# A hybrid attention and delta-rule layer on one Trainium2 core: level zero of the recurrence ahead of the last convolution taps, the last root on VectorE, weight splits in three parts

## The reference, cut to what matters

```python
h = rms_norm(x, norm_g)
proj = h @ w_in                                  # mixers' inputs, and 3 x 1024 merge gates
# A: top-128 keys by an indexer, softmax attention over them
# B: causal conv (4 taps) + silu on q, k, v; gated delta rule in chunks:
a_mat = where(strict, (k_beta @ k.T) * decay, 0)
t_inv = triangular_solve(eye + a_mat, eye)       # inverse of a unit triangular matrix
v_new = t_inv @ (...) ; o = q @ state + attn @ v_new ; state = decay * state + k.T @ v_new
o_b   = rms_norm(o, b_out_norm) * silu(b_z)
# C: compressed + selected + window attention, each gated
merged = g_a * (y_a @ wb_a) + g_b * (y_b @ wb_b) + g_c * (y_c @ wb_c)
out = x + merged @ w_out
```

## Time and profile before

| | us |
|---|---|
| median of 3 runs (lowest, highest) | 652.02 (651.27, 655.02) |
| the profiled execution: its time, its span | 654.71, 652.6 |
| busy: TensorE, VectorE, ScalarE, GpSimd | 589.1 (90%), 394.3 (60%), 333.5 (51%), 222.6 (34%) |
| granted TensorE clock, mean over the span | 0.974 |
| chain that ended last | PE 67%, DVE 14%, ACT 8%, issue 5%, POOL 2%, DMA 2% |

### The profile page before, as it was taken

How to read it: one execution, slowest core, us unless ns; L and a number is a source line. 1 busy time by engine, 2 the same in 40 slices (tenths; PEclk the granted TensorE clock), 3 DMA queues, 4 the chain that set the end, 5 groups by cost and what they waited for, 6 DMA issues and landing times.

```text
span 652.6 us, 10019 instructions
## 1 busy us (share of the span) xinstructions
PE 589.1 (90%) x3763; PEld 368.8 (57%) x3763; DVE 394.3 (60%) x889; ACT 333.5 (51%) x585; POOL 222.6 (34%) x161
## 2 busy tenths in 40 slices
PE   3969988999999996999999999988988799799998
PEld 2424556756548653677677777754554466333443
DVE  6401487451687965786876557447799765577311
ACT  4625654425688768350812525346766677243510
POOL 0133453333044466042531530422221464242520
PEclk9998999989999899799999999979999999999999
DMA  8254764443113232120211110111120211162411
GB/s 321 63 127 111 155 123 130 138 153 113 51 50 113 66 98 65 33 65 2 65 33 32 53 46 1 46 53 51 36 78 34 66 33 43 56 228 74 145 55 48
DMA packets 31168, 53.04 MB, mean 81 GB/s; under 512 B 2743, under 2 KB 13201, under 8 KB 31121
## 3 DMA queue, kind: packets, MB, share of 16 engines
q1 hardware_dynamic: 30961, 52.27, 27.7%
q10 hardware_dynamic: 160, 0.14, 0.1%
HBM read 49.98 MB, written 2.42 MB: 80 GB/s over the span
## 4 chain that ended last, share of the span: by engine, by line
PE 67%; DVE 14%; ACT 8%; issue 5%; POOL 2%; DMA 2%; SPq 2%; DVEq 0%; ACTq 0%; PEldq 0%; POOLq 0%
PE bank L1790 12%; PE bank L1603 10%; PE bank L1605 9%; PE bank L1604 9%; PE bank L1858 5%; PE bank L1860 5%; PE bank L1862 5%; ACT stage L735 3%; PE bank L1639 2%; DMA stage<-in_w_in 2%; PE bank L1682 2%; POOL w_lo L518 1%; PE bank L1988 1%; PE bank L1821 1%; PE bank L1761 1%
## 5 line engine op out<-in xcount | busy, mean ns | idle before, releaser
L518 POOL TENSOR_TENSOR w_lo<-stage,w_hi 128x1024 f16<-128x1024 f32 (+4 forms) x76 | 149.1, 1964 | 250.9 <-ACT w_hi L743 250.9
L1790 PE MATMUL bank<-work 128*128 128x128 f32 x616 | 80.1, 280 | 8.1 <-DVEq L1298 7.8
L1790 PEld LDWEIGHTS bank<-work 128*128 128x128 f32 x616 | 77.7, 195 | 17.1 <-DVEq L1298 9.9
L743 ACT ACTIVATE w_hi<-stage 128x1024 f16<-128x1024 f32 (+4 forms) x76 | 74.5, 981 | 18.8 <-issue 14.4
L735 ACT ACTIVATE stage<-stage,small 128x512 f32<-128x512 f32 (+4 forms) x120 | 73.6, 662 | 8.1 <-DMA stage<-in_w_in 8.0
L1858 PE MATMUL bank<-hT_hi,w_hi 128*128 128x512 f16 x192 | 74.5, 388 | 1.7 <-PE bank L1862 0.9
L1860 PE MATMUL bank<-hT_lo,w_hi 128*128 128x512 f16 x192 | 74.2, 387 | 0.5 <-PE bank L1605 0.2
L1862 PE MATMUL bank<-hT_hi,w_lo 128*128 128x512 f16 x192 | 74.1, 386 | 0.3 <-PE bank L1605 0.2
L1603 PE MATMUL bank<-w_hi,hT_hi 128*128 128x260 f16 (+4 forms) x192 | 62.7, 327 | 9.1 <-POOL w_lo L518 6.4
L1604 PE MATMUL bank<-w_lo,hT_hi 128*128 128x260 f16 (+4 forms) x192 | 62.5, 326 | 0.0
L1605 PE MATMUL bank<-w_hi,hT_lo 128*128 128x260 f16 (+4 forms) x192 | 62.5, 325 | 0.0
(11 more groups left out here) (319 smaller groups left out, 1183.6 us busy)
## 6 DMA issues: line engine op xcount, KB each, us to landing
stage<-in_w_in SPq DMA_DIRECT2D x40, 512.0 KB, 3.5
stage<-in_c_phi_w SPq DMA_DIRECT2D x8, 512.0 KB, 4.0
stage<-in_w_branch SPq DMA_DIRECT2D x8, 512.0 KB, 3.7
stage<-in_w_out SPq DMA_DIRECT2D x8, 512.0 KB, 3.8
stage<-in_w_in SPq DMA_DIRECT2D x8, 260.0 KB, 2.8
strips<-rel_rows SPq DMA_DIRECT2D x8, 256.0 KB, 7.3
late<-in_x SPq DMA_DIRECT2D x1, 2048.0 KB, 10.1
out_x<-late SPq DMA_DIRECT2D x8, 256.0 KB, 2.0
```

Source lines behind the costliest of these rows:

```text
L518: gp.tensor_tensor(piece_view(w_lo[:, k % PAIRS, :], c), piece_view(stage[:, piece_at[c, j] % STAGES, :], c), piece_view(w_hi[:, k % PAIRS ...
L743: nc.scalar.activation(piece_view(w_hi[:, k % PAIRS, :], c), full, ACT.Copy).then_inc(hi_ready, 1)
L1790: ins = mm(ps[:, h * P:(h + 1) * P], lhs(h), rhs(h), start=True, stop=True)
```

## The change

Seven edits.

- **Level zero first.** The four transposes `("n", 0)` move from behind the fill at the head of the recurrence into the last tile of B2, behind its fifth step. On VectorE `decayed_products(0)` and `level_zero(0)` stand before convolutions 9, 10, 11, whose taps become a generator at the head of `topk_last`, taken one at a time in levels 1 to 3; four top-k steps stand before `decayed_products(0)`, eight more before the log decays. On ScalarE the SiLUs of 9 to 11 and the first tap of 11 move behind the three gate SiLUs (L907).
- **token_major(0)** moves from level 3 to level 5.
- **The last root** (`("ob", 3)`) is found on VectorE from a bit pattern and three Newton steps (`bit_root`, 13 small instructions), and the whole last norm moves from ahead of unit 0 into unit 2.
- **Entry of the attention:** the compressed products move into unit 0, and 12 fill steps (`FILL_FIRST`, three times 4) stand among them; block 3 units have 4 fill steps and not 5.
- **Splits in three parts:** ScalarE scales row 0, row 1 and rounds in three different units; GpSimd's part follows the rounding.
- **finish(g)** a unit earlier (`u % 4 == 2`), without the copy L1493.
- **Top-k rounds** of the attention by `ROUNDS_AT`, from unit 3 on, 7 in 8 units.

```diff
-TOPK_0, TOPK_A, TOPK_B = 10, 16, 6
+TOPK_0, TOPK_A, TOPK_B, TOPK_C = 10, 24, 6, 4
-ATTENTION_FILL = (7, 7, 5, 5)
+ATTENTION_FILL = (7, 7, 5, 4)
+FILL_FIRST = 4
+ROUNDS_AT = (1, 1, 0, 1, 2, 1, 0, 1)
...
-        def attention_splits(u):
-            g = 12 + u // 4
-            c = GATE_CHUNKS[g // 4]
-            if g % 4 == 3:
-                return [(after(c), 2 + u % 4 - 1)] if u % 4 in (1, 2) else []
-            return [(after(c), g % 4)] if u % 4 == 3 and g % 4 < 2 else []
+        SPLIT_PARTS = {0: (0, "row0"), 1: (0, "row1"), 2: (0, "hi"), 4: (1, "row0"), 5: (1, "row1"), 6: (1, "hi"),
+                       8: (2, "row0"), 9: (2, "row1"), 10: (3, "row0"), 12: (3, "row1"), 13: (2, "hi"), 14: (3, "hi")}
+        def attention_split(u):
+            j, part = SPLIT_PARTS.get(u % 16, (None, None))
+            return after(GATE_CHUNKS[3 + u // 16]), j, part
...
-                else:
+                elif t < 3:
                     first_tap(8 + t)
-                silus(t, {1: (8,), 2: (9,), 3: (10, 11)})
+                silus(t, {1: (8,)})
...
             ins.then_inc(z_ready, 1)
+            silu_conv(9)
+            first_tap(11)
+            silu_conv(10)
+            silu_conv(11)
...
-            sqrt(("ob", NT - 1), ss_o[:, 4 * NT - 4:4 * NT], 4)
...
+            def bit_root(ss, n):
+                y, w = root[:, 0:n], newton[:, 0:n]
+                bits = y.bitcast(i32)
+                hold(ve.tensor_scalar(bits, ss.bitcast(i32), 1, None, ALU.arith_shift_right))
+                hold(ve.tensor_scalar(bits, bits, -1.0, ROOT_SEED, ALU.mult, ALU.add))
+                for n in range(3):
+                    hold(ve.tensor_tensor(w, y, y, ALU.mult))
+                    hold(ve.tensor_tensor(w, w, ss, ALU.mult))
+                    hold(ve.tensor_scalar(w, w, -0.5, 1.5, ALU.mult, ALU.add))
+                    if n < 2:
+                        hold(ve.tensor_tensor(y, y, w, ALU.mult))
+                return y, w
...
             difference(0)
             conv(8)
-            conv(9)
+            for _ in range(TOPK_C):
+                next(topk_last)
             decayed_products(0)
-            conv(10)
             level_zero(0)
-            conv(11)
+            topk_last = chain(conv_taps(9), conv_taps(10), conv_taps(11), topk_last)
...
-                elif m == "sel":
-                    hold(ve.tensor_copy(oc, o_cg[:, 4 * q:4 * q + 4, :]))
                 if m != "A":
+                    before = o_cg[:, 4 * q:4 * q + 4, :] if m == "sel" else oc
...
-            for _ in output_norm(NT - 1):
-                pass
-            cmp_out()
-            last_rounds = topk(3)
             for u in range(len(units)):
                 if u + 2 < len(units):
                     logits(u + 2)
                 probs_lo(u)
-                next(last_rounds, None)
+                if u == 0:
+                    cmp_out(0)
+                elif u == 1:
+                    cmp_out(1)
+                elif u == 2:
+                    for _ in output_norm(NT - 1):
+                        pass
+                    last_rounds = topk(3)
+                else:
+                    for _ in range(ROUNDS_AT[u % 8]):
+                        next(last_rounds, None)
                 for f in Y_EARLY.get(u, ()):
                     y_lo(f)
-                if u % 4 == 3 and u >= 7:
+                if u % 4 == 2 and u >= 6:
                     finish(u // 4 - 1)
...
+                if (t, k) == (3, 4):
+                    GD.wait(pe, ("nnt", 0))
+                    transposes(("n", 0), [neg_nT[:, h, :] for h in range(4)])
...
             fill(2 * FILL_T)
-            GD.wait(pe, ("nnt", 0))
-            transposes(("n", 0), [neg_nT[:, h, :] for h in range(4)])
...
-                    if l == 3 and c == 0:
+                    if l == 5 and c == 0:
                         pe.wait_ge(conv_done, 12)
                         token_major_inputs(0)
...
             unit_logits(0)
+            fill(FILL_FIRST)
             unit_logits(1)
+            fill(FILL_FIRST)
...
                 if u + 2 < len(units):
                     unit_logits(u + 2)
+                if u == 0:
+                    compressed_out(0)
+                    fill(FILL_FIRST)
+                    compressed_out(1)
```

More of the change, by code:

```diff
@@ L691, in _ @@
             for u in range(len(units)):
-                for c, j in attention_splits(u):
+                c, j, part = attention_split(u)
+                if part == "hi":
                     lo_split(c, j)
@@ L1208, in conv @@
                         hold(ins)
-                ins.then_inc(conv_ready, 1)
+                    else:
+                        ins.then_inc(conv_ready, 1)
+                    yield
+            def conv(m):
+                for _ in conv_taps(m):
+                    pass
             for t in range(4):
@@ L1336, in output_norm @@
                 hold(ve.tensor_reduce(so, o_sq, AX.X, ALU.add))
-                ve.tensor_scalar(so, so, 1.0 / B_HD, EPS, ALU.mult, ALU.add).then_inc(ROOT_IN.sem, 1)
-                yield
-                y, w = newton_root(("ob", c), so, 4)
+                ins = ve.tensor_scalar(so, so, 1.0 / B_HD, EPS, ALU.mult, ALU.add)
+                if c < NT - 1:
+                    ins.then_inc(ROOT_IN.sem, 1)
+                    yield
+                    y, w = newton_root(("ob", c), so, 4)
+                else:
+                    hold(ins)
+                    y, w = bit_root(so, 4)
                 yield
```

51 lines of the change are left out of this document (36 added, 15 removed).

## The result

The changed kernel takes 656.56 us (median of 15 runs, 653.81 to 657.66), the kernel before on the same chip 652.56 (15 runs). The ratio is 1.0046, 95% interval 1.0033 to 1.0060: slower by 3.0 us by the ratio and by 4.0 between the medians, which by the ratio is just within the 0.5% that a measurement can tell from no change; the whole interval lies above 1, so the change does not gain. Forecast were 640.7 us, a gain of 11.3. The profiled execution of the changed kernel took 656.08 (span 654.0).

The account below looks back on a forecast made before the run. TensorE, busy 90% of the span, was taken as the bound, VectorE in units 16 to 31. Gains 6.7 + 2.0 + 2.6 = 11.3 us from the median 652.0 gave 640.7; 631 to 646 held about 0.82.

Parts of the forecast that it names:

- The entry with units 0 and 1: Start of the attention: 4.9 us of waits and slow clock removed, 0.4 added waiting for the first exponential.
- slow units 0 and 1: Attention entry: 6.5 us at mean clock 0.54 hold 3.5 of full clock, so 2.9 us removed.
- Part A: Level zero first, between B2 and the recurrence: gain of 6.7 us (4 to 9).
- the gain of A comes back in B2: Rival: extra top-k delays log decays, TensorE waits in B2: 644 us; 0.22 shared with the clock rival.
- Part C: The attention's units 8 to 47: gain of 2.6 us, summed from −3.4, +0.3, +2.5 and +3.2.
- waits of pieces 2 and 3: Units 13 and 14: TensorE waits 2.3 and 2.5 us for late-rounded pieces, together 4.8 lost.
- The blocked product: Small VectorE product of `finish` beside GpSimd's rest: 0.8 us each in units 6, 18, 22, 34 (bounds 0 and 1.8).
- Units 32 to 47: Last units: some 4.5 us of waits, leaving one blocked `finish` 0.8 and 0.5 at the end: gain 3.2.
- Part B: Entry of the attention and the moved norm: 4.9 − 2.9 = 2.0 us gained, if the clock stays up.
- the clock falls again at the entry: Rival: a slow stretch like the old one at the attention's entry, 2.9 us, 643.6; 0.22 shared with the B2 rival.
- The norm: Unit 2, VectorE, 4.4 us at one go: TensorE waits 2.5 for `probs_lo(3)` in unit 4 (bounds 1 and 3.5).
- Slower than before: Rival: scattered waits keep the clock at 1.2 GHz, deciding above 23 us there; 30 us gives 656; chance 0.03.

Follow-up runs that it names:

- ac_gate: Parts A and C on the kernel before, with ScalarE draining gate tile 0 ahead of the split queued with it: 643.04 us, ratio 0.9849.
- A and C: The changed kernel with Part B undone (norm and root ahead of the units, no FILL_FIRST): 644.84 us, ratio 0.9875.
- no lead: The changed kernel without the 12 FILL_FIRST fill steps, ATTENTION_FILL back to 7, 7, 5, 5: 651.63 us, ratio 0.9983.
- products first: The changed kernel with both groups of narrow compressed products ahead of unit 0, the last FILL_FIRST between them: 652.38 us, ratio 0.9989.
- norm in unit 0: The changed kernel with the last norm in unit 0, not unit 2 (also written norm_u0): 654.18 us, ratio 1.0005.
- table early: The changed kernel with one small exponential on ScalarE behind the last cp drain, to load the table early: 653.67 us, ratio 0.9994.
- pieces early: The changed kernel with the split parts of pieces 2 and 3 of the first block moved to units 8 to 12: 654.47 us, ratio 1.0006.
- late `finish`: finish back at u % 4 == 3: in the changed kernel 651.18 us, ratio 0.9971; added to ac_gate 637.01 us, ratio 0.9739.
- A alone: Only Part A on the kernel before, attention entry and units as before: 647.73 us, ratio 0.9918.
- A and B: The changed kernel with Part C undone (whole splits, copy kept, a top-k round a unit, finish a unit later): 659.38 us, ratio 1.0096.
- ac_lead: ac_gate with late `finish`, 10 fill steps moved to the entry from units 32 to 41, pieces 2 and 3 split early: 635.19 us, ratio 0.9704.

## Why the prediction was wrong

Predicted 640.7, with a range of 631 to 646; measured 656.6, or 652.02 × 1.0046 = 655.0 from the median that the forecast started from, a miss of 14.3 us. "Slower" and "the same" together had a chance of 0.08. Two of the three parts came out near their sums (A 1.4 under, C 0.2 to 0.7 over, C partly by luck); B has the miss of 13 to 14.

**The steps that failed.** Profile against profile, the miss is 12.7 (641.3 forecast for the span of 654.0), and it lies in three places. *The entry with units 0 and 1* was put at 4.9 − 0.4 = 4.5 shorter and is 16.91 − 12.79 = 4.1 longer: the term "slow units 0 and 1" was taken as removed on the condition that the clock stays up, and the clock was 0.70; the table load was in no term. *Units 32 to 46* were put at 3.2 shorter and are 0.6 longer (37.38 for 36.80). *The tail* is 1.6 longer at a low clock that no term had. What is left, among it the 1.6 won ahead of B2's last tile, makes −1.3.

**Part A: 6.7 forecast, 5.3 measured by the ratio (4.9 between the medians), 6.2 by both traces up to the first logits.** Right step by step. The wait in B2, ahead of the `n` transposes at 250.79, was 0.61 (forecast 0.5); VectorE's product ended at 249.95 + 0.69 = 250.64, 1.5 earlier than forecast, and TensorE was there earlier by as much. Level 1 starts at 254.80 and runs at the full clock (its matmuls of 512 columns start 0.215 apart). The bank wait of gate tile 0 was 2.12, forecast 2.1, and its cause, ScalarE's order, is shown by ac_gate. The rival "the gain of A comes back in B2" is out.

**Part C: 2.6 forecast, 2.8 and 3.3 measured, and yet wrong inside.** The forecast had −4.8 for the waits of pieces 2 and 3 in it. They came (2.38 and 2.48, for 2.3 and 2.5), but they belong to B's lead: with A and C alone they are absent. C by itself was thus forecast at 7.4 and gave 2.8; that the sum of 2.6 was met is luck. Two steps failed, and a stretch at the low clock came on top (0.92 over the 20.96 of units 16 to 23 in A and C, some 1.7; with gate tile 0 drained first the same units take 19.39 at 1.00):
- *The blocked product.* It was priced at 0.8 in four places, 3.2. All six candidates were hit, with 10.13 − 6 × 0.166 = 9.1 us more on VectorE (1.74 + 1.33 + 1.72 + 1.66 + 2.07 + 1.61 = 10.13), and removing them is worth 4.9 to 7.2. The mechanism was right; the value was taken in the lower half of its bounds, as if the two might miss each other. They don't: in every kernel with the rounding and `finish` in the same six units (A and C, no lead, products first, norm in unit 0, table early, gate tile first) the six products last 1.3 to 2.1. In the code both hang on the same unit's transposes. It is timing all the same: in "pieces early" piece 3 is rounded in unit 12 and the product of unit 14 takes 0.17, and in unit 10, where piece 2's rounding and `finish` now meet, the product (462.19) starts 0.04 before GpSimd's rest (462.23) and takes 0.17 too. The Trainium skill, page "SBUF — State Buffer", section "Who interferes with whom", has an exclusive lock for the pair; by the page alone each would cost up to the whole 2.13, and the six, 1.33 to 2.07, lie nearer to that than to my 0.8. The trace agrees with the page.
- *Units 32 to 47 at +3.2.* They gave −0.9 in A and C (20.15 to 21.05 in 32 to 39, and 16.65 both times in 40 to 46). The forecast took the waits "behind the finish of the top-k" as gone, and did not ask when the top-k ends: with 7 rounds in 8 units the 32 steps last to unit 36, and from unit 3 on to unit 37; before, they ended in unit 31. That is by the code; in the windows of units 32 to 39 VectorE does one step of the top-k before, five in A and C and seven in the changed kernel, 0.68 each. VectorE's busy time in units 32 to 39 went from 12.79 to 17.10 and to 18.48. The late `finish` brings the stretch to 19.02 and VectorE's busy time to 14.90.

Units 24 to 31 were forecast at +2.5 and gave 3.2, as VectorE's row said.

**Part B: 2.0 forecast, −11.2 to −11.6 measured.** With the waits for the pieces booked here, forecast −2.8. Its terms, from the windows of A and C against those of the changed kernel:
- *The entry, forecast 4.5 shorter.* Against A and C it is 16.91 − 12.66 = 4.25 longer, so the step has a miss of 8.75. An estimate of its terms from the first window: the clock, 16.91 × (1 − 0.70) = 5.1, forecast 0; idle time, 16.91 − 15.46 = 1.45, forecast 0.4; and the 12 fill steps, 12 × 0.214 = 2.6, forecast as covered. The rival "the clock falls again at the entry" was priced at 2.9, as a stretch like the old one; it happened, and was longer than the old one (0.70 over 16.91 against 0.73 over 12.79). The narrow products took 2.98 + 3.67 = 6.65 where 32 in one go took 3.78 in A alone: 2.9. The first exponential stood behind its table load of 1.28, which starts only when its logits are there. Undoing the order alone gave 3.7 by the ratio; its stretch up to unit 2 is 3.2 shorter, as no lead's is 3.2 longer than that of A and C (15.87 and 12.66).
- *The 12 fill steps themselves.* Priced at nothing ("a hole that four fill steps cover", "1.7 of the old 23.9 were fill steps that moved"). The entry is 1.04 shorter without them (no lead), since 1.5 of their 2.6 fill idle time; given back are 0.5 in units 40 to 46 and 0 to 0.65 in 24 to 31. So the price of nothing was right to within half a us. What they cost is the two waits for pieces 2 and 3, which they pull forward; those were forecast, but not as B's.
- *The norm.* A wait of 2.25, forecast 2.5, and right in cause: norm_u0 removes 2.26. What was not seen is that 7.9 us of idle time lay on VectorE in unit 0, ahead of the place where it was put.
- *Units 8 to 15:* 25.67 − 19.10 = 6.57, of it 4.86 the two waits, forecast 4.8; the rest is mostly a stretch at the low clock directly behind them (0.94 over 8 to 15, an estimate of 1.5), which no term had.
- Back comes 2.2 in units 16 to 23, where A and C had its own low stretch (0.92) and a blocked product.

4.25 + 2.26 + 6.57 − 2.22 + 0.04 + 0.22 − 0.54 = 10.6, and 1.0 outside these stretches: 11.6, the difference of the two profiled spans (654.0 − 642.4). The medians stand 11.7 apart.

**The rivals.** "Slower than before" named the clock alone, decided above 23 us at the low level. That count did not come: by the mean clocks of the windows about 13.6 us of the stretch from 419.15 to 494.17 lay at the low level (2 × 0.30 × 16.91, 2 × 0.06 × 25.67, 2 × 0.01 × 18.74), worth 6.8. It was more than half of the way, though, and joined by what had no rival with a chance of its own: an uncovered table load and a top-k that ends late, at nothing in the sum, and `finish` blocked at six places of six, priced low. The range's lower side was filled with waits being absent; but the waits of A, of the pieces and of the norm were all there, at their size to within 0.3 us.

**Open:** why the clock falls where it does in the entry. The same order on TensorE took 15.37 at a mean of 0.78 (norm in unit 0), 16.91 at 0.70 (changed kernel, A and B) and 18.32 at 0.64 (pieces early, late `finish`), one profiled execution each, and the narrow products in them took 1.99 to 3.14 and 2.96 to 3.67. So the slow time at the entry isn't set by the order alone, and how much of B's 11.7 another execution would show is not settled. The executions of norm_u0 and table_early spread over 8.6 and 10 us, those of A and C over 0.7. By the ratios the single repairs of 4.1 (no lead), 3.7 (products first), 2.7 (norm) and 3.4 (table) sum to 13.9, more than B's 11.2; at equal clock they sum to 9.7 to 11.6, and products first and table early remove the same wait. No run separates the bit root from the move of the norm, or in C the parts of the splits from the direct use of `o_cg`.

## What to carry to other kernels

Filler work that is moved has two prices, one at each end: read how much idle time it lands in (here 1.5 of 2.6), and from what stretch it is taken; one whose TensorE row is nearly full gave back 1.26 of 1.7 (ac_lead), one bound by VectorE 0 to 0.65 of 1.7. A stream that runs ahead brings forward the deadline of all that feeds it, so move the feeding with it. Where two engines' instructions hang on the same event and one blocks the other in a trace, price the block at nearly its full length for each place, unless the order of their starts is known. And a slow stretch that a trace shows is not removed by removing one wait ahead of it: put what the clock does in the new order into the sum, at its full price, until a run shows otherwise.
